# A mixture-of-experts stage with small blocks: their rows turned one run ahead, the loops turned round, weight loads released one by one, operands at multiples of 64 bytes

## What is computed

```python
def expert_mlp(xb, w1, w3, w2):
    return (jax.nn.silu(xb @ w1) * (xb @ w3)) @ w2
# w1, w3: 1024 x 512, w2: 512 x 1024 for each of 32 experts, all fp32
# rows are sorted by expert, each expert's rows are cut into blocks of 128 (EXPERT_BLK)
return jnp.zeros((T, D), h.dtype).at[tok_s].add(w_s[:, None].astype(h.dtype) * y_assign)
```

## Time and profile before

| | |
|---|---|
| median of three runs | 2371.46 us (2365.16 to 2383.85) |
| the profiled execution | 2364.32 us, span 2362.8 us |
| PE busy in the span | 1990.6 us (84%) |
| DVE, ACT, POOL busy | 1612.0, 1074.3, 568.7 us |
| stage of the experts | from about 1352 to about 2253 us of the span |
| full blocks, small blocks | 40, 10 |
| DMA | 553.53 MB, mean 234 GB/s |

### The profile page before, as it was taken

How to read it: one execution, slowest core, us unless ns; L and a number is a source line. 1 busy time by engine, 2 the same in 40 slices (tenths; PEclk the granted TensorE clock), 3 DMA queues, 4 the chain that set the end, 5 groups by cost and what they waited for, 6 DMA issues and landing times. The chain is left out here.

```text
span 2362.8 us, 40338 instructions
## 1 busy us (share of the span) xinstructions
PE 1990.6 (84%) x12996; PEld 1597.2 (68%) x12997; DVE 1612.0 (68%) x3110; ACT 1074.3 (45%) x2054; POOL 568.7 (24%) x562
## 2 busy tenths in 40 slices
PE   5999999997999986539999489899899998999910
PEld 3788888886777775328888367777677776777710
DVE  2568888887666665748998658664436664648768
ACT  2311111123777786024444157554446554547533
POOL 1024444450111111203565311100101011010066
PEclk7999999998999999769999689999899999999955
DMA  8855555554555475856778179875566786759777
GB/s 278 275 193 195 196 198 197 196 198 140 194 158 175 139 238 188 302 185 198 256 254 274 55 281 379 311 280 214 187 231 240 279 312 235 285 216 373 288 288 291
DMA packets 220937, 553.53 MB, mean 234 GB/s; under 512 B 28429, under 2 KB 43365, under 8 KB 219688
## 3 DMA queue, kind: packets, MB, share of 16 engines
q1 hardware_dynamic: 176464, 435.12, 52.4%
q0 software_dynamic: 25360, 76.08, 8.8%
q10 hardware_dynamic: 19024, 41.18, 5.0%
HBM read 457.25 MB, written 167.63 MB: 264 GB/s over the span
## 5 line engine op out<-in xcount | busy, mean ns | idle before, releaser
L2374 DVE TENSOR_TENSOR LO<-WIDE,HI 128x2048 fp32r<-128x2048 f32 x128 | 284.5, 2283 | 15.5 <-ACT HI L2303 15.5
L596 DVE SCALAR_TENSOR_TENSOR ARENA<-ARENA,TAPW 128x512 f32<-128x512 f32 (+3 forms) x493 | 293.3, 672 | 0.0
L2303 ACT CAST HI<-WIDE 128x2048 fp32r<-128x2048 f32 x128 | 240.1, 1908 | 55.0 <-DMA WIDE<-in_w_expert_gate 33.1
L422 POOL TENSOR_TENSOR MS<-SSQ,K 128x1 f32<-128x1 f32 x17 | 170.0, 9999 | 289.0 <-ACT H L465 289.0
L2374 DVE TENSOR_TENSOR LO<-W2E,HI 128x2048 fp32r<-128x2048 f32 x64 | 143.6, 2284 | 84.9 <-ACT HI L2303 84.9
L715 PE MATMUL PJ<-WIN_H,HTH 128*128 128x512 f32 x680 | 172.5, 396 | 15.0 <-ACT HTH L471 11.7
L1026 ACT ACTIVATE PR<-SBX,NM 128x256 f32<-128x256 f32 (+1 forms) x384 | 171.9, 455 | 1.9 <-DVE NM L960 1.1
L719 PE MATMUL PJ<-WIN_H,HTL 128*128 128x512 f32 x680 | 168.4, 390 | 0.0
L723 PE MATMUL PJ<-WIN_L,HTH 128*128 128x512 f32 x680 | 168.0, 389 | 0.0
L497 ACT ACTIVATE ARENA<-PJ 128x512 f32<-128x512 f32 x51 | 30.4, 598 | 290.8 <-PE PJ L723 290.8
L715 PEld LDWEIGHTS PJ<-WIN_H,HTH 128*128 128x128 f32 x680 | 127.2, 189 | 46.1 <-ACT HTH L471 15.9
...
...
## 6 DMA issues: line engine op xcount, KB each, us to landing
...
```

The costliest lines, as they stand in the source:

```text
L422: pool.tensor_tensor(MS[:], SSQ[:], const("eps"), ALU.add).then_inc(ms_ready, 1)
L596: ins = nc.vector.scalar_tensor_tensor(out=out, in0=src, scalar=tap, in1=out, op0=ALU.mult, op1=ALU.add)
L2303: nc.scalar.copy(HI[n][:, cols], raw[n][:, cols]).then_inc(hi_ready[n], 1)
L2374: nc.vector.tensor_tensor(LO[n][:, cols], raw[n][:, cols], HI[n][:, cols], ALU.subtract).then_inc(lo_ready[n], 1)
```

## The change

- **Rows turned a run ahead.** PE turns the rows of the next run's small block inside the small block before, between BE and GP (`turn_small(n + 1)`), and ACT copies them there (`take_small`). The first small block has buffers and semaphores of its own (IDX0, XG0). POOL fetches the rows a run earlier, too.
- **Loops turned round.** A run is now a small block and then its experts, on PE and POOL; the last expert is in the loop. `experts_table` makes the head of each run by another formula (one tensor_tensor over 128x1024 fewer), with an end mark, and a copy of the heads that is held at 31. ACT and DVE keep their loops.
- **Weight loads released step by step.** In SP's loop the wait on `sy_done` becomes one for each weight: W1 waits for `sa_done`, W3 for `sb_done`, W2 for `sy_done`. The first load of W2 waits for the first small block's rows and no longer for the first full block's.
- **Waits moved.** PE waits for the last block's `y_taken` only ahead of YP, for `xl_ready` ahead of the turned rows (no longer at the small block's start), and `block_` has one more wait (`sx_ready`) ahead of turning rows.
- **Addresses.** IDX now stands ahead of W2E, and the small index tiles behind SEL and BASE; so HI, LO, W2E, XS, GTS and XGS start at multiples of 64 bytes. MT_H and MT_L stay where they were against 64.

The core of the diff:

```diff
-                    then(stt(HEAD[:], RUN[:], 1.0, SMALL1[:], ALU.add, ALU.mult))
-                    then(nc.vector.tensor_scalar(HEAD[:], HEAD[:], -1.0, None, ALU.add))
-                    then(nc.vector.tensor_tensor(square, numbers[:, :, None].to_broadcast([P, NEXP, NEXP]), HEAD[:, None, :].to_broadcast([P, NEXP, NEXP]), ALU.is_equal))
-                    then(nc.vector.tensor_tensor(square, square, numbers[:, None, :].to_broadcast([P, NEXP, NEXP]), ALU.mult))
-                    then(nc.vector.tensor_reduce(FIRST[:], square, AX.X, ALU.add))
+                    then(stt(INDEX[:], RUN[:], -1.0, SMALL1[:], ALU.add, ALU.add))
+                    then(nc.vector.tensor_tensor(square, INDEX[:, None, :].to_broadcast([P, NEXP, NEXP]), numbers[:, :, None].to_broadcast([P, NEXP, NEXP]), ALU.is_lt))
+                    then(nc.vector.tensor_reduce(HEADS_[:, 0:NEXP], square, AX.X, ALU.add))
+                    then(nc.vector.tensor_scalar(HEADS_[:, NEXP:], HEADS_[:, 0:1], 0.0, float(NEXP), ALU.mult, ALU.add))
                     then(stt(state["unit"][:], FROM[:], float(P // T), RUN[:], ALU.mult, ALU.add))
-                    then(nc.vector.tensor_copy(entries(0), FIRST[:]))
...
         W1, W3 = (state["wide"][:].rearrange("p (n k f) -> p n k f", n=2, f=DEXP)[:, n] for n in range(2))
-        W2 = sb("W2E", [P, KF, D])
+        IDX, W2 = sb("IDX", [P, 1], I32), sb("W2E", [P, KF, D])
         fetching, turning, ended = sem("fetching"), sem("turning"), sem("rows_ended")
-        IDX, XG, XH, XL = sb("IDX", [P, 1], I32), sb("XG", [P, D]), sb("XH", [P, KD, P], F32R), sb("XL", [P, KD, P], F32R)
+        XG, XH, XL = sb("XG", [P, D]), sb("XH", [P, KD, P], F32R), sb("XL", [P, KD, P], F32R)
         S, G, GH, GL, Y = sb("SE", [P, DEXP]), sb("GE5", [P, DEXP]), sb("GH", [P, KF, P], F32R), sb("GL", [P, KF, P], F32R), sb("YE", [P, D])
-        IDXS, XGS, XS = sb("IDXS", [T, 1], I32), sb("XGS", [T, D]), sb("XS", [P, KD, T])
+        XGS, XS = sb("XGS", [T, D]), sb("XS", [P, KD, T])
...
-            return entry(engine, 0, g, 0, LAST - 1), entry(engine, 0, g + 1, 1, LAST)
+            return entry(engine, 0, g, 0, LAST), entry(engine, 0, g + 1, 1, NEXP)
         raw = [w.rearrange("p k n -> p (k n)") for w in (W1, W3, W2[:])]
...
-                sp.wait_ge(x_in, 16)
+                sp.wait_ge(first_x_in, 16)
                 for half in range(2):
                     sp.dma_start(half_of(W2[:], half), half_of(w2[0], half)).then_inc(w2_in[half], 16)
                 with sp.Fori(1, NEXP) as e:
                     split = sp.snap(e * 2)
-                    sp.wait_ge(sy_done, entry(sp, 4, e, 1, LAST))
+                    smalls = entry(sp, 4, e, 1, LAST)
                     for n, (dst, src, come) in enumerate(weights):
+                        sp.wait_ge((sa_done, sb_done, sy_done)[n], smalls)
                         for half in range(2):
                             sp.wait_ge(lo_ready[n], sp.snap(split - 1) if half == 0 else split)
                             sp.dma_start(half_of(dst, half), half_of(src[ds(e, 1)].rearrange("a p k f -> (a p) k f"), half)).then_inc(come[half], 16)
...
-                    pool.wait_ge(sx_turned, n + 1)
+                    slot = place(e * CAP, T)
+                    pool.wait_ge(sx_turned, n)
                     pool.sem_inc(fetching, 1)
                     pool.dma_start(IDXS[:], dr["slot"][ds(slot, T), :]).then_inc(sidx_in, 16)
-                    pool.wait_ge(sidx_in, n * 16 + 16)
+                    pool.wait_ge(sidx_in, n * 16)
                     pool.sem_inc(fetching, 1)
                     pool.indirect_dma_start(XGS[:], None, dr["h2"], bass.IndirectOffsetOnAxis(ap=IDXS[:].bitcast(U32), axis=0)).then_inc(sx_in, 16)
-                fetch_small(0, 0)
-                pool.dma_start(IDX[:], dr["slot"][T:T + P, :]).then_inc(idx_in, 16)
-                pool.wait_ge(idx_in, 16)
-                gather(0)
-                pool.wait_ge(x_in, 16)
-                end = bounds(pool, 0)[1]
-                with pool.If(end > 1):
-                    with pool.Fori(1, end) as b:
-                        fetch(0, 0, T, b)
-                number = runs(pool)
-                with pool.Fori(0, number) as g:
+                pool.dma_start(IDX0[:], dr["slot"][0:T, :]).then_inc(first_idx_in, 16)
+                pool.wait_ge(first_idx_in, 16)
+                pool.indirect_dma_start(XG0[:], None, dr["h2"], bass.IndirectOffsetOnAxis(ap=IDX0[:].bitcast(U32), axis=0)).then_inc(first_x_in, 16)
+                with pool.Fori(0, pool.snap(runs(pool) + 1)) as g:
                     head, behind = run(pool, g)
-                    fetch_small(behind, g + 1)
-                    with pool.Fori(pool.snap(head + 1), pool.snap(behind + 1)) as e:
+                    fetch_small(entry(pool, 5, g + 1, 0, LAST), g + 1)
+                    with pool.Fori(head, behind) as e:
                         first, end = bounds(pool, e)
...
                                               skip_runtime_bounds_check_because="an expert has P rows of its own and no more others than tokens, or a small block")
+                def take_small(n):
+                    if isinstance(n, int) and n == 0:
+                        act.wait_ge(first_turned, 1)
+                    else:
+                        act.wait_ge(sx_turned, n + 1)
+                    nc.scalar.copy(XS[:], XPS).then_inc(sx_ready, 1)
                 def small(e, n, meanwhile=None):
                     row = 0 if isinstance(e, int) else out_row(entry(act, 1, e, 0, MAXBLK) * P + n * T, T)
-                    act.wait_ge(sx_turned, n + 2)
-                    nc.scalar.copy(XS[:], XPS).then_inc(sx_ready, 1)
                     act.wait_ge(sa_done, n + 1)
                     nc.scalar.activation(SS[:], APS, ACT.Silu).then_inc(ss_ready, 1)
+                    act.wait_ge(sg_turned, n + 1)
+                    nc.scalar.copy(GTS[:].rearrange("p k t -> p (k t)"), GPS).then_inc(sgt_ready, 1)
+                    take_small(n + 1)
                     if meanwhile is not None:
                         meanwhile()
...
-                def small(e, n, meanwhile=None):
-                    pe.wait_ge(sx_in, n * 16 + 16)
-                    if not isinstance(e, int):
-                        first = entry(pe, 1, e, 1, MAXBLK)
-                        pe.wait_ge(xl_ready, first + 1)
+                def turn_small(n):
+                    first = isinstance(n, int) and n == 0
+                    if first:
+                        pe.wait_ge(first_x_in, 16)
+                    else:
+                        pe.wait_ge(sx_in, n * 16)
                     pe.sem_inc(turning, 1)
                     for k in range(KD):
-                        mm = nc.tensor.transpose(XPS[:, k], XGS[:, k * P:(k + 1) * P], const("ident")[0:T, 0:T])
-                    mm.then_inc(sx_turned, 1)
+                        mm = nc.tensor.transpose(XPS[:, k], (XG0 if first else XGS)[:, k * P:(k + 1) * P], const("ident")[0:T, 0:T])
+                    mm.then_inc(first_turned if first else sx_turned, 1)
+                def turn_small_g(n):
+                    pe.wait_ge(sg_ready, n + 1)
+                    nc.tensor.transpose(GPS, GS[:], const("ident")).then_inc(sg_turned, 1)
+                def small(e, n):
+                    static = isinstance(e, int)
                     for half in range(2):
                         pe.wait_ge(w1_in[half], e * 16 + 16)
                         pe.wait_ge(w3_in[half], e * 16 + 16)
                     pe.wait_ge(sx_ready, n + 1)
-                    if not isinstance(e, int):
+                    if not static:
+                        first = entry(pe, 1, e, 1, MAXBLK)
                         pe.wait_ge(s_ready, first + 1)
                         pe.wait_ge(g_ready, first * 2 + 2)
                     on_groups(APS, XS, W1, KD).then_inc(sa_done, 1)
                     on_groups(BPS, XS, W3, KD).then_inc(sb_done, 1)
-                    if meanwhile is not None:
-                        meanwhile()
-                    if not isinstance(e, int):
+                    if static:
+                        turn_small_g(n)
+                        turn_small(n + 1)
+                        pe.wait_ge(x_in, 16)
+                        pe.wait_ge(sx_ready, n + 2)
+                        turn_x(range(KD)).then_inc(x_turned, 1)
+                    else:
+                        pe.wait_ge(xl_ready, first + 1)
+                        turn_small(n + 1)
                         pe.wait_ge(gl_ready, first * 2 + 2)
-                        pe.wait_ge(y_taken, first * 2 + 2)
-                    pe.wait_ge(sg_ready, n + 1)
-                    nc.tensor.transpose(GPS, GS[:], const("ident")).then_inc(sg_turned, 1)
+                        turn_small_g(n)
                     for half in range(2):
                         pe.wait_ge(w2_in[half], e * 16 + 16)
+                    if not static:
+                        pe.wait_ge(y_taken, first * 2 + 2)
```

(13 more changed lines are left out.)

27 lines of the change are left out of this document (15 added, 12 removed).

## The result

The changed kernel takes 2341.07 us (median of four, 2337.89 to 2346.88); the kernel before took 2370.28 us beside it (median of four). The ratio is 0.9869, 95% interval 0.9845 to 0.9894: 29 us faster, inside the range of 2299 to 2349, but of the 46 to 48 us forecast only some 60% came. It lies above the 2308 to 2336 us that the bounds of the forecast's own parts gave together; only the allowance for the rivals covers it. The profiled execution has a span of 2339.2 us against 2362.8.

What follows compares the result with a forecast made beforehand. PE was taken to bound the experts' full blocks, with about 11 of 40 bound by DMA too. Terms summed to 45.7 us, giving 2318 (profiled execution) or 2326 (median); predicted 2322 us, range 2299 to 2349.

Steps and rivals of the forecast that it cites:

- the addresses: Experts' full blocks: operands at multiples of 64 bytes save 0.46 us in each of 29 blocks, 13.3 us; bounds 0 and 18.4.
- the low clock: At a full block's start behind a small one: less PE idling recovers a third of the loss, 2 us; bounds 0 and 6.
- the early release: Weight loads released earlier at small blocks: less PE idling in rows of one-block experts, 1.5 us; bounds 0 and 4.
- POOL: Two runs with one full block: POOL's gather comes late behind the turning, -2 us for both; bounds 0 and -6.
- The start: First full block's rows fetched 8 us later, against W2 about 5 us earlier: -1.5 us; bounds -4 and +1.
- The table: Experts table: loses one step of 1.23 us, gains two small ones; worth 1 us.
- 1 (addresses worth nothing): Rival: the step of eight matmuls differs between stages for something other than addresses; 2335 us, chance 0.18.
- 2 (the gap moved): Rival: loop entry and its loads still cost 2.4 us behind the small block's YP; 2337 us, chance 0.12.
- 4 (DMA takes more): Rival: all one-block experts, 25 of 40 blocks, keep their old pace; 2333 us, chance 0.09.
- 18.3 + 5.1 - 16 + 9 + 15: Nine small blocks: XS wait gone, old GS wait gone, new GS wait, low clock in AE/BE hidden, gap behind YP shortened.
- 3 (DMA gives way): Rival: earlier loads keep one-block experts fed, all forty blocks gain, first run's stalls go; 2311 us, chance 0.11.
- 5: Rival: POOL's gather comes late in every run, so PE waits inside the small block; 2394 us, chance 0.05.

Runs made afterwards that it cites:

- product_early: Changed kernel, but in each run's last block DVE makes only W1's low part before the small block's GS, W3's after it; 2328.3 us, ratio 0.9831.
- all_best: Changed kernel with POOL's order mixed, expert 0's W3 split early, W3's low part behind GS, and MT_H, MT_L at multiples of 64 bytes; 2301.4 us, ratio 0.9710.
- old_addresses: Changed kernel with HI, LO, W2E, XS, GTS and XGS back at 32 bytes past a multiple of 64; 2350.1 us, ratio 0.9925.
- align_only: Kernel before with only the addresses changed (IDX ahead of W2E, IDXS behind BASE); 2355.7 us, ratio 0.9940.
- release_late: Changed kernel with all six weight loads waiting for the small block's end (sy_done) again; 2337.9 us, ratio 0.9881.
- experiment 6: Changed kernel, but ACT and DVE split expert 0's W3 ahead of the first small block's work; 2334.0 us, ratio 0.9852.
- rows_first: Changed kernel, but POOL fetches a run's first full block's rows ahead of the next small block's; 2331.8 us, ratio 0.9842.

## Why the prediction was right, and where its sizes were off

Where the 46 us went, by the cuts of the stage: inside the nine small blocks 31.4 were forecast and 29.7 came. In the runs 14.8 were forecast (13.3 for the addresses, 2 for the low clock, 1.5 for the early release, less 2 for POOL) and 3.5 came. The start was charged with a loss of 1.5, and the first small block lost 3.3. The table's 1 us came. So the direction and the mechanisms were right, and the shortfall is for the most part one term, POOL's: 9.7 of the 11.3 us missing in the runs stand in the two one-block runs. That the time still fell inside the range owes something to the width that rivals 1, 2 and 4 had given it, and none of these three is what happened.

*The small blocks: right.* The terms inside the nine (18.3 + 5.1 - 16 + 9 + 15) make 31.4 us; measured are 29.7. The gap behind YP is 0.45 us or none (2.37), AE steps by 1.77 in all nine, and the new wait for GS, 13.7 us in nine against the 16 charged, is there for the reason foreseen; product_early shows it by removing it. What was left out: behind the wait for GS the granted clock is low, and it now falls on YP of the small block. The stretches of 4 us around YP (columns as in the earlier trace rows), first in the changed kernel:

```profile
1885.00:1889.00 4.00, 4.00 (x36) 2.41 (x28) 0.00 (x0) 0.37 (x1) 0.00 (x0) 0.57 1.00 363
```

and then in product_early:

```profile
1871.50:1875.50 4.00, 3.55 (x39) 2.46 (x40) 3.45 (x2) 0.44 (x2) 0.00 (x0) 1.00 0.84 308
```

A mean of 0.57 is nearly the lower of the two levels, 1.2 of 2.4 GHz. From YP's start to the full block's start the nine take 26.2 us, at product_early's 2.38 each it would be 21.4. The term "low clock at a block's start, a third of 6" was about right: the first eight matmuls behind the nine small blocks took 23.6 us before and take 21.0. The 9 us for the low clock in AE and BE were read from two of the six places; the six together are 7.8.

*The addresses: the size right, the rule and the blocks wrong.* 13.3 us were charged, on the sentence "the eleven blocks that DMA holds get nothing". By the ratios it is 14 us alone and 13 beside the new order. But the blocks are not those: the first run's six gained nothing, and the one-block experts in a row of the later runs gained as the others did. What failed was to take a DMA share of 1.03 for a bound: the share stays there while the rate goes from 381 to 402 GB/s. Reading 1.86 in the output projection as the price of one operand off 64 was wrong too; it was the right pair of numbers with the wrong address rule, and all_best contradicted it. The changed kernel gained because its padding happens to put the pairs alike beyond a multiple of 256. Behind the row: the Trainium skill, TensorE: Matmul & The Clock Gate, Part 1, gives N / 2.4 GHz plus about 2.5 ns, 216 ns for 512 columns, without a term for addresses; for these fp32r products the runs disagree, with 227 ns at the best and 234 where the pair is unlike.

*POOL: the step that failed.* "-2 for both" one-block runs, bounds 0 to -6: by old_addresses against before it is -11.0, by the changed kernel against align_only -11.7. POOL behind the turning of a small block's rows in the changed kernel, against the earlier trace rows:

```profile
1666.41 0.55 POOL L2265 DMA_DIRECT2D IDXS<-slot_tokens  x1 [21.47 <-PE XP L2475]
1672.34 0.88 POOL L2268 DMA_INDIRECT XGS<-h_rows,IDXS  x1 [5.38 <-DMA IDXS<-slot_tokens]
1674.97 0.57 POOL L2256 DMA_DIRECT2D IDX<-slot_tokens  x1 [1.76 <-issue]
1679.45 1.82 POOL L2252 DMA_INDIRECT XG<-h_rows,IDX  x1 [3.90 <-DMA IDX<-slot_tokens]
```

The chain of two lists and two gathers takes 13.0 us from start to start, not the 9.5 of the earlier trace rows: the wait for the second list is 3.90 us and not 2.65, and that for the first 5.38. The cause is the weight loads that now run at that moment (release_late above: the same first list takes 2.08 us with the queues empty). It holds in all fourteen traces: of the waits for a list, the 112 during which DMA moved under 60 GB/s took 1.6 to 2.7 us, the 182 at 350 GB/s and more took 4.7 to 7.6. The 9.5 us of the earlier trace rows had been read in a quiet place. And what PE then has to wait is followed by the low clock:

```profile
1687.31 1.30 PE L2438 MATMUL XP<-K,XG 128*128 128x128 f32 x6 [3.35 <-DMA XG<-h_rows,IDX]
...
1689.59 2.75 PE L2454 MATMUL YP<-HI,GH 128*128 128x512 f32 x8
1692.17 1.98 PE L2454 MATMUL YP<-HI,GL 128*128 128x512 f32 x8
```

This run is 5.7 us longer than in align_only (24.1 and 18.4): 3.35 of it are this wait, 1.0 the low clock at the block's start, and the rest nearly all the low clock in XP and YP behind the wait. The text had the right queue and the right victim, and the sum took over a duration that did not hold in the new order.

*The start.* -1.5 was charged, bounds -4 and +1; the first small block takes 3.3 us more. The wait for the full block's rows is there:

```profile
1380.89 1.97 PE L2438 MATMUL XP<-K,XG 128*128 128x128 f32 x8 [7.46 <-DMA XG<-h_rows,IDX]
1382.79 2.41 PE L2463 MATMUL YP<-W2E,GTS 128*32 128x256 f32 x32
1387.80 3.41 PE L2449 MATMUL AE<-HI,XH 128*128 128x512 f32 x8 [2.60 <-issue]
```

It replaces W2's 5.9 us, and the gap behind YP is still 2.60 us here; that the loads of the first block's bounds could not run ahead is my reading and wasn't tried. That the first run shows nothing of the address gain (117.8, before 116.8) is not due to the late start, since align_only, which starts as before, shows nothing either (116.6). It is the weights' late arrival of experiment 6: rows_first, with the same addresses, takes 109.2.

*The early release: +1.5 charged*, and nothing of it shows in the stage.

*The table: 1 us charged, 1.0 measured.* From the start of the output projection's last matmul to the stage's start it is 38.1 us before and in align_only, which has the old table, and 37.1 in the changed kernel (37.0 to 37.7 in the others). The part ahead of the stage is all the same 5.8 us longer in the changed kernel's profiled execution (1357.9 against 1352.1 us), but the distance is there already at the output projection's first matmul (1055.8 and 1047.5 us), up to which the change does nothing but move tiles; in the other kernels the stage starts between 1354 and 1365 us. This scatter is why the profiled executions are only 24 us apart with stages 30 us apart.

*The rivals.* 1 (addresses worth nothing), 2 (the gap moved) and 4 (DMA takes more) are refuted by align_only, by the 0.45 us gaps and by the two stretches at 399 and 402 GB/s (of 4's blocks only the first run's stayed at the old pace). 3 (DMA gives way) was right for the one-block experts of the later runs, which gain like the others, and wrong for the first run, whose stalls stayed (117.8 us). 5 was right that a fetch would be late, but at full blocks of one-block runs and not inside the small ones.
